# Eight modulation blocks as 1024 columns of four row groups instead of 512 columns of eight, in a one-core transformer trunk

## The chip, the cores and the metric

One Trainium2 (trn2) chip, one of its cores. The metric is the device time of one execution in microseconds (us). The engines are named as in the profile: PE is TensorE (the matmuls; PEld its weight loads), DVE is VectorE, ACT is ScalarE, POOL is GpSimd, SP is SyncE, whose queue issues most of the transfers. SPq and ACTq are the transfer-issuing instructions of SP and ACT.

## The reference

One layer of a streaming encoder on 512 tokens of 1024 channels, all float32. The change touches only the first line of it:

```python
mod = silu(c) @ w_ada + b_ada                 # c: 1 x 1024, w_ada: 1024 x 6144
sh1, sc1, g1, sh2, sc2, g2 = split(mod, 6)    # six rows of 1024
h = rms_norm(x) * (1 + sc1) + sh1
proj = h @ w_in                               # 1024 x 1696
gm  = gmlp(proj[:, :1024])                    # u and v halves, v is layer-normed and mixed over positions
mla = attention(proj[:, 1024:])               # q and kv latents (672 columns), 8 heads
x = x + g1 * (concat(rms_norm(gm), rms_norm(mla)) @ w_out)
x = x + g2 * moe(rms_norm(x) * (1 + sc2) + sh2)   # 64 experts, top 8, and a shared one
```

## The kernel before, in words

There is no planner. Each engine has its own program, written out in order, and engines wait for each other on semaphores that count completed steps. Tokens are worked on in four tiles of 128 (t = 0 to 3); the 1024 channels are eight row groups of 128 (c = 0 to 7).

**The modulation.** `w_ada` is 24 MB, twelve blocks of 2 MB. Partition p holds rows 8p to 8p+7 of it, so one block is eight multiply-adds of DVE (a column of `silu(c)` times a row group, added to an accumulator), after which a matmul with a matrix of ones on PE sums the accumulator over the 128 partitions (`ada_sum`, L611) and ACT copies the sum from its PSUM bank into the row `mod` (`copy_mod`, L1000). The first four blocks (`first_block`, L1322) make `sh1` and `sc1`. They are already cut as 1024 columns of four row groups, and are summed differently, into columns. The other eight (`ada_block`, L1375) are 512 columns of all eight row groups; two of them make one row of `mod`. These eight are numbered 0 to 7 in what follows, and the four rows of `mod` that they make (gate 1, shift 2, scale 2, gate 2) are rows 0 to 3. Rows of `mod` are used only from the scaling of `w_out` on (L519) and later. But PE waits once for all eight copies ahead of the up-projections (L675), ACT waits for all eight blocks ahead of its latent casts (L1087), POOL ahead of its key copies (L513), and SP ahead of the load of `w_u` (L419), since memory is shared.

**The order around it.** From about 40 us to 120 us the engines run side by side:

- PE (L647 to L671): the latent projections, two to a tile of tokens (512 and 160 columns; eight accumulating matmuls each), then the v projections, one of 512 columns to a tile, then 20 transposes of the latents. The eight `ada_sum` stand among them: one behind the first projection of tiles 1, 2 and 3, one behind the last latent projection, and one behind each of the four v projections. Projection i waits until the result of projection i-4 has been copied out of its bank (L633: `proj_ok` at least i-3, i counted from 0; so the seventh, i = 6, needs the third copy).
- ACT (L1050 to L1088): the copies of these results, `copy_mod` behind the same projections, ten small loads that it issues itself behind tile 0 (`load_smalls`, L1033), the scaling of the latents, casts of the weights to reduced precision (L1072), GELU of v, the casts `latT_high`.
- DVE (L1400 to L1433): block 0, then for each tile one block and the squares of the tile's latents (`lat_sums`, L1391), then blocks 5 to 7, the low parts of the weights (L1414), statistics of v, and `latT_low` (L1431), for which PE waits at L674.
- SP (L407 to L420): the load of each block waits until the block that used its buffer three blocks ago is done (L410). A load of 2 KB of `b_ada` follows each. `w_v`, `w_q`, `w_kv` are loaded in between.
- An accumulator may be written again when PE has summed it (L1380), a bank when ACT has copied it (L616).

From 120 us on come the up-projections, attention, the output projection, routing, and from about 340 us the 64 experts, which take two thirds of the time and which the change doesn't touch.

Of the kernel before, what the change touches and what calls it, by code (L numbers as in the profile page):

```python
# [46 lines left out]
def trunk_kernel(nc, a, out):  # L47
# [31 lines left out]
    with ExitStack() as ctx:  # L79
# [20 lines left out]
        w_lat = at("w_lat_sb", 72, [P, C, LAT])  # L100
        ada_w = [at(f"ada_w{i}", kb, [P, C, BANK]) for i, kb in enumerate((94, 110, 40))]
        h = at("h_sb", 126, [P, T, D])
# [3 lines left out]
        acc_g1 = at("acc_g1", 28, [P, D])  # L106
        bias0 = [at(f"bias0_{i}", kb, [P, BANK]) for i, kb in enumerate((163, 165, 16))]
        u = at("u_sb", 16, [P, T, GW])
# [112 lines left out]
        cact = small("cact", [P, C])  # L221
        acc = [small(f"ada_acc{i}", [P, BANK]) for i in range(3)]
        ss = small("ss", [P, T])
# [9 lines left out]
        ws_raw = small("ws_raw", [P, GG, GB])  # L233
        lsq = at("lsq", 18, [P, QL])
        ws_low = small("ws_low", [P, GG, GB])
# [119 lines left out]
        def ada_buffer(j):  # L355

            n = j - ADA_FIRST
            return n % 3, 32 * (n // 3 + 1) + 16

# [32 lines left out]
        def _(sp):  # L392
# [14 lines left out]
            for j in range(ADA_FIRST, ADA):  # L407
                i, _ = ada_buffer(j)

                sp.wait_ge(ada_dve, (1, 2, 4)[i] if j < ADA_FIRST + 3 else j - 2)  # L410
                sp.dma_start(ada_w[i][:], w_ada_v[:, :, j * BANK:(j + 1) * BANK]).then_inc(ld_ada[i], 16)
                sp.dma_start(bias0[i][0:1, :], a["b_ada"][:, j * BANK:(j + 1) * BANK]).then_inc(ld_ada[i], 16)
                if j == ADA_FIRST + 2:
                    sp.dma_start(w_v[:], w_in_v[:, :, GW:2 * GW]).then_inc(ld["wv"], 16)
                if j == ADA_FIRST + 4:
                    sp.wait_ge(hT_tr, 2 * T)
                    sp.dma_start(w_q[:], a["w_q_up"][0].rearrange("(p c) n -> p c n", c=QC)).then_inc(ld["wq"], 16)
                    sp.dma_start(w_kv[:], a["w_kv_up"][0].rearrange("(p c) n -> p c n", c=KC)).then_inc(ld["wq"], 16)
# [69 lines left out]
        def _(pool):  # L488
# [15 lines left out]
            pool.memset(bias0[0][:], 0.0)  # L504
            pool.memset(bias0[1][:], 0.0)
            pool.memset(bias0[2][:], 0.0).then_inc(bias_zero, 1)
            pool.wait_ge(ld["ws"], 16)
# [87 lines left out]
        def _(pe):  # L595
# [14 lines left out]

            def ada_sum(j):  # L611

                n = j - ADA_FIRST
                pe.wait_ge(acc_ok, n + 1)
                if n >= 2:
                    pe.wait_ge(mod_ok, n - 1)  # L616
                pe.matmul(bank[j % 2][:], ones[:], acc[n % 3][:], start=True, stop=True).then_inc(ada_mm, 1)

# [30 lines left out]
            for t in range(T):  # L649
                for m, (n0, n1) in enumerate(lat_cuts):  # L650
                    projection(t * NL + m, t, w_lat, n0, n1)
                    if t and m == 0:
                        ada_sum(ADA_FIRST + t - 1)
                if t == 2:
# [3 lines left out]
                    last.then_inc(wsT_tr, 1)  # L658
            ada_sum(ADA_FIRST + T - 1)
            pe.wait_ge(ld["wv"], 16)  # L660
            for t in range(T):
                projection(V0 + t, t, w_v, 0, GW)
                ada_sum(ADA_FIRST + T + t)

# [325 lines left out]
        def _(act):  # L990
# [8 lines left out]

            def copy_mod(j):  # L1000
                act.wait_ge(ada_mm, j - ADA_FIRST + 1)
                act.copy(mod[:, j // 2, j % 2 * BANK:(j % 2 + 1) * BANK], bank[j % 2][:]).then_inc(mod_ok, 1)

# [46 lines left out]
            for t in range(T):  # L1050
                for m, (n0, n1) in enumerate(lat_cuts):
                    i = t * NL + m
                    act.wait_ge(proj_mm, i + 1)
                    act.copy(lat[:, t, n0:n1], bank[2 + i % 4][:, 0:n1 - n0]).then_inc(proj_ok, 1)
                    if t and m == 0:
                        copy_mod(ADA_FIRST + t - 1)
                if t == 0:
                    load_smalls()
            copy_mod(ADA_FIRST + T - 1)
            act.wait_ge(stats_ok, 1)  # L1060
# [17 lines left out]
            for t in range(T):  # L1078
                gelu(v, V0 + t, t)
                copy_mod(ADA_FIRST + T + t)  # L1080

# [230 lines left out]
        def _(dve):  # L1312
# [62 lines left out]
            def ada_block(j):  # L1375
                n = j - ADA_FIRST
                buf, loads = ada_buffer(j)
                dve.wait_ge(ld_ada[buf], loads)
                if n >= 3:
                    dve.wait_ge(ada_mm, n - 2)  # L1380
                w = ada_w[buf]
                link(dve.scalar_tensor_tensor(acc[n % 3][:], w[:, 0, :], cact[:, 0:1], bias0[buf][:], ALU.mult, ALU.add))
                for c in range(1, C):
                    ins = dve.scalar_tensor_tensor(acc[n % 3][:], w[:, c, :], cact[:, c:c + 1], acc[n % 3][:], ALU.mult, ALU.add)
                    if c < C - 1:
                        link(ins)
                ins.then_inc(acc_ok, 1)
                dve.wait_ge(acc_ok, n + 1)
                dve.engine_nop().then_inc(ada_dve, 1)
# [410 lines left out]
```

## Time and profile before

| | |
|---|---|
| three runs | 1049.43, 1050.78 (median), 1052.73 us |
| the profiled execution | 1044.55 us, of which the span of its trace is 1042.7 us |
| mean granted clock of PE | 0.975 of full speed |
| busy, share of the span | PE 90%, DVE 84%, ACT 59%, POOL 30% |
| instructions | 14345, of which DVE 1306 |
| q1 (SP's transfers) | 73344 packets, 252.23 MB |
| q10 (ACT's transfers) | 4064 packets, 0.94 MB |

The profile is of one execution. "Busy" counts the time in which an engine has an instruction in work. Idle time ahead of an instruction is given with what ended it (the releaser); "issue" stands where the engine waited for nothing that the profile shows. The chain of waits is the work that ended last, followed back from the end.

### The profile page before, as it was taken

The page shows a single profiled execution, that of the slowest core. Times are in us where ns is not written, and L with a number is a line of the kernel's source. Part 1 is how long each engine was busy: PE and PEld are TensorE (multiplying, and loading weights), DVE is VectorE, ACT ScalarE, POOL GpSimd, SP SyncE. Part 2 cuts the span into 40 slices and gives each one's busy share as a digit, 9 for nine tenths or more (in the row PEclk, how much of TensorE's full clock was granted, in tenths as well). Part 3 has the DMA queues.
Part 4 walks back from the last instruction along what each step waited for, and adds up shares of the span by engine and source line. Part 5 has one row for each costly group of instructions (what it writes and reads, how often), then busy time and mean ns, then how long its engine had stood idle before and what let it go on. Part 6 is the DMA issues. An engine that isn't in the chain of part 4 may idle for free.

```text
span 1042.7 us, 14345 instructions
## 1 busy us (share of the span) xinstructions
PE 940.5 (90%) x4323; PEld 734.3 (70%) x4324; DVE 870.9 (84%) x1306; ACT 612.0 (59%) x969; POOL 316.3 (30%) x193
## 2 busy tenths in 40 slices
PE   1899999899998989989999999999999999889984
PEld 1654674678897567778777777777777777777773
DVE  4888883456668379989999999999899999899895
ACT  4215462563041467767777777777776767677671
POOL 1000206980001123333433424333323243332422
PEclk9899999899999989999999999999999999999997
DMA  9996220202194989999999999999999999999972
GB/s 350 397 375 234 81 81 1 111 1 82 60 337 164 271 248 349 377 356 320 349 351 353 361 346 366 354 359 346 326 363 329 320 374 352 366 348 366 339 251 28
DMA packets 96497, 290.46 MB, mean 279 GB/s; under 512 B 20520, under 2 KB 21032, under 8 KB 95824
## 3 DMA queue, kind: packets, MB, share of 16 engines
q1 hardware_dynamic: 73344, 252.23, 64.5%
q0 software_dynamic: 19056, 36.89, 14.9%
q10 hardware_dynamic: 4064, 0.94, 0.4%
q8 instruction: 16, 0.26, 0.1%
q14 instruction: 17, 0.14, 0.0%
HBM read 284.60 MB, written 39.98 MB: 311 GB/s over the span
## 4 chain that ended last, share of the span: by engine, by line
DMA 38%; PE 33%; DVE 13%; issue 9%; ACT 4%; POOL 2%; POOLq 0%; SPq 0%; DVEq 0%; ACTq 0%
DMA out<-oute,src_tab 23%; DMA xe<-h_rows,src_tab 9%; PE bank L637 6%; PE bank L598 5%; PE bank L600 5%; PE bank L599 5%; DMA w_gu<-in_w_exp_up 4%; DVE gu_low L1626 3%; PE bank L710 3%; POOL out L553 2%; PE bank L879 2%; DVE oute L1662 2%; PE bank L753 2%; PE bank L863 1%; PE bank L770 1%
## 5 line engine op out<-in xcount | busy, mean ns | idle before, releaser
L1626 DVE TENSOR_TENSOR gu_low<-w_gu,gu_high 128x1024 fp32r<-128x1024 f32 x256 | 301.3, 1219 | 17.3 <-ACT gu_high L1209 13.7
L1209 ACT CAST gu_high<-w_gu 128x1024 fp32r<-128x1024 f32 x256 | 256.5, 1055 | 63.7 <-PE bank L600 42.4
L553 POOL DMA_INDIRECT out<-oute,src_tab x64 | 135.8, 2122 | 419.0 <-DMA out<-oute,src_tab 255.5
L598 PE MATMUL bank<-gu_high,xeT_high 128*128 128x512 f32 x512 | 207.4, 405 | 3.7 <-DVE xeT_low L1626 3.6
L600 PE MATMUL bank<-gu_high,xeT_low 128*128 128x512 f32 x512 | 201.5, 394 | 0.0
L599 PE MATMUL bank<-gu_low,xeT_high 128*128 128x512 f32 x512 | 201.1, 393 | 0.0
L1626 DVE TENSOR_TENSOR d_low<-w_d,d_high 128x1024 fp32r<-128x1024 f32 x128 | 150.5, 1217 | 1.8 <-ACT d_high L1215 1.8
L1215 ACT CAST d_high<-w_d 128x1024 fp32r<-128x1024 f32 x128 | 128.2, 1054 | 14.5 <-PE bank L600 11.5
L598 PE MATMUL bank<-d_high,hwT_high 128*128 128x512 f32 x256 | 109.6, 428 | 7.8 <-DVE hwT_low L1626 7.8
L598 PEld LDWEIGHTS bank<-gu_high,xeT_high 128*128 128x128 f32 x512 | 96.6, 189 | 26.0 <-issue 5.8
L600 PEld LDWEIGHTS bank<-gu_high,xeT_low 128*128 128x128 f32 x512 | 96.3, 188 | 22.3
L547 POOL DMA_INDIRECT xe<-h_rows,src_tab x64 | 98.7, 1542 | 43.4 <-DVE src_tab L1696 19.2
L599 PEld LDWEIGHTS bank<-gu_low,xeT_high 128*128 128x128 f32 x512 | 96.5, 188 | 19.5
L879 PE MATMUL bank<-ident,xe 128*128 128x128 f32 x512 | 72.9, 287 | 38.7 <-DMA xe<-h_rows,src_tab 38.4
L879 PEld LDWEIGHTS bank<-ident,xe 128*128 128x128 f32 x512 | 65.3, 194 | 56.4 <-issue 50.8
L600 PE MATMUL bank<-d_high,hwT_low 128*128 128x512 f32 x256 | 104.1, 407 | 0.0
L1626 DVE TENSOR_TENSOR xeT_low<-bank,xeT_high 128x512 fp32r<-128x512 f32 x128 | 82.1, 683 | 25.6 <-ACT xeT_high L1225 25.3
L599 PE MATMUL bank<-d_low,hwT_high 128*128 128x512 f32 x256 | 103.2, 403 | 0.0
L1225 ACT CAST xeT_high<-bank 128x512 fp32r<-128x512 f32 x128 | 68.9, 591 | 46.4 <-PE bank L879 46.4
L1662 DVE TENSOR_TENSOR oute<-bank,mod_rows 128x512 f32<-128x512 f32 x128 | 82.1, 683 | 9.4 <-PE bank L600 9.4
L598 PEld LDWEIGHTS bank<-d_high,hwT_high 128*128 128x128 f32 x256 | 50.6, 198 | 16.9 <-issue 5.1
L600 PEld LDWEIGHTS bank<-d_high,hwT_low 128*128 128x128 f32 x256 | 50.0, 195 | 11.7
(284 smaller groups left out, 1289.6 us busy)
## 6 DMA issues: line engine op xcount, KB each, us to landing
w_gu<-in_w_exp_gate SPq DMA_DIRECT2D x128, 512.0 KB, 6.2
w_gu<-in_w_exp_up SPq DMA_DIRECT2D x128, 512.0 KB, 11.2
w_d<-in_w_exp_down SPq DMA_DIRECT2D x128, 512.0 KB, 7.5
ada_w<-in_w_ada SPq DMA_DIRECT2D x8, 2048.0 KB
first_w<-in_w_ada SPq DMA_DIRECT2D x3, 2048.0 KB, 22.8
w_out_sb<-in_w_out SPq DMA_DIRECT2D x2, 2048.0 KB, 7.6
w_lat_sb<-in_w_in SPq DMA_DIRECT2D x1, 2688.0 KB, 23.2
x_sb<-in_x SPq DMA_DIRECT2D x1, 2048.0 KB, 13.7
```

The costliest lines, as they stand in the source:

```text
L547: pool.indirect_dma_start(xe[i][:], None, h2_dram, bass.IndirectOffsetOnAxis(ap=rows, axis=0), bounds_check=last_row, oob_is_err=False).th ...
L553: pool.indirect_dma_start(out_rows, bass.IndirectOffsetOnAxis(ap=rows, axis=0), oute[i][:], None, bounds_check=last_row, oob_is_err=False, ...
L598: pe.matmul(dst, xh, wh, start=start, stop=False)
L599: pe.matmul(dst, xh, wl, start=False, stop=False)
L600: return pe.matmul(dst, xl, wh, start=False, stop=stop)
L637: last = pe.matmul(bank[2 + i % 4][:, 0:n1 - n0], hT[:, c, t * P:(t + 1) * P], w[:, c, n0:n1], start=(c == 0), stop=(c == C - 1))
L879: last = pe.transpose(bank[c // 4][:, c % 4 * P:(c % 4 + 1) * P], xe[b][:, c:D:C], ident[:])
L1209: act.copy(gu_high[half][:, m], w_gu[half][i][:, m]).then_inc(gu_high_ok[half], 1)
L1215: act.copy(d_high[:, m], w_d[i][:, m]).then_inc(d_high_ok, 1)
L1225: act.copy(xeT_high[i][:, m * HC:(m + 1) * HC, :], bank[m][:].rearrange("p (c n) -> p c n", c=HC)).then_inc(xe_high_ok, 1)
L1626: return dve.tensor_tensor(low, whole, high.bitcast(F32), ALU.subtract)
L1662: last = dve.tensor_tensor(oute[i][:, cols], bank[4 + m][:], mod[:, GATE2, cols], ALU.mult)
```

## The change

Blocks 0 to 7 become 1024 columns of four row groups. Blocks 2r and 2r+1 are the two halves of the sum for row r of `mod`, in one accumulator of 1024 columns. A row of `b_ada` comes with the even block. Per block, DVE has four multiply-adds on 128x1024 in place of eight on 128x512. Each load of 2 MB reads runs of 4 KB in place of 2 KB. PE sums a whole row at once (`ada_sums(r)`: two matmuls, one for each 512 columns, into banks 0 and 1), and ACT copies it with two copies. The eight sums stand at four places in place of eight: behind the first projection of tile 2, behind the last latent projection, and behind the v projections of tiles 1 and 3. The accumulators move to the first 8 KB of each partition, where `x` was, and the small tensors behind them move down by 6 KB.

The diff (buffers and functions whole, nothing else was changed):

```diff
--- before.py
+++ after.py
@@ -98,13 +98,14 @@
         w_u = at("w_u_sb", 40, [P, C, GW])
         w_v = at("w_v_sb", 56, [P, C, GW])
         w_lat = at("w_lat_sb", 72, [P, C, LAT])
-        ada_w = [at(f"ada_w{i}", kb, [P, C, BANK]) for i, kb in enumerate((94, 110, 40))]
+        ada_w = [at(f"ada_w{i}", kb, [P, HK, D]) for i, kb in enumerate((94, 110, 40))]
         h = at("h_sb", 126, [P, T, D])
         hT = at("hT", 143, [P, C, S])
         first_w = [at(f"first_w{i}", kb, [P, HK, D]) for i, kb in enumerate((94, 110, 167, 40))]
         acc_sh1 = at("acc_sh1", 159, [P, D])
         acc_g1 = at("acc_g1", 28, [P, D])
-        bias0 = [at(f"bias0_{i}", kb, [P, BANK]) for i, kb in enumerate((163, 165, 16))]
+        bias0 = [at(f"bias0_{i}", kb, [P, D]) for i, kb in enumerate((163, 16))]
+        acc = [at(f"ada_acc{i}", 4 * i, [P, D]) for i in range(2)]
         u = at("u_sb", 16, [P, T, GW])
         v = at("v_sb", 167, [P, T, GW])
         vn = at("vn_sb", 175, [P, T, GW])
@@ -219,7 +220,6 @@
         freq = small("freq", [P, RH])
         cT = small("cT", [P, C])
         cact = small("cact", [P, C])
-        acc = [small(f"ada_acc{i}", [P, BANK]) for i in range(3)]
         ss = small("ss", [P, T])
         lnst = small("lnst", [P, T * GG, 6])
         lnmv = small("lnmv", [P, T * GG, 2])
@@ -231,7 +231,7 @@
         ln_g = small("ln_g", [P, GW])
         ln_b = small("ln_b", [P, GW])
         ws_raw = small("ws_raw", [P, GG, GB])
-        lsq = at("lsq", 18, [P, QL])
+        lsq = at("lsq", 20, [P, QL])
         ws_low = small("ws_low", [P, GG, GB])
         bsT = small("bsT", [P, GG])
         qa_g = small("qa_g", [P, QC])
@@ -355,7 +355,7 @@
         def ada_buffer(j):
 
             n = j - ADA_FIRST
-            return n % 3, 32 * (n // 3 + 1) + 16
+            return n % 3, 16 + sum(16 + 16 * (b % 2 == 0) for b in range(n % 3, n + 1, 3))
 
         def shared_banks(t):
 
@@ -408,8 +408,10 @@
                 i, _ = ada_buffer(j)
 
                 sp.wait_ge(ada_dve, (1, 2, 4)[i] if j < ADA_FIRST + 3 else j - 2)
-                sp.dma_start(ada_w[i][:], w_ada_v[:, :, j * BANK:(j + 1) * BANK]).then_inc(ld_ada[i], 16)
-                sp.dma_start(bias0[i][0:1, :], a["b_ada"][:, j * BANK:(j + 1) * BANK]).then_inc(ld_ada[i], 16)
+                s, k0 = divmod(j, 2)
+                sp.dma_start(ada_w[i][:], w_ada_v[:, k0 * HK:(k0 + 1) * HK, s * D:(s + 1) * D]).then_inc(ld_ada[i], 16)
+                if k0 == 0:
+                    sp.dma_start(bias0[s % 2][0:1, :], a["b_ada"][:, s * D:(s + 1) * D]).then_inc(ld_ada[i], 16)
                 if j == ADA_FIRST + 2:
                     sp.dma_start(w_v[:], w_in_v[:, :, GW:2 * GW]).then_inc(ld["wv"], 16)
                 if j == ADA_FIRST + 4:
@@ -502,8 +504,7 @@
             pool.iota(part[:], pattern=[[0, 1]], base=0, channel_multiplier=1, allow_small_or_imprecise_dtypes=True).then_inc(consts, 1)
 
             pool.memset(bias0[0][:], 0.0)
-            pool.memset(bias0[1][:], 0.0)
-            pool.memset(bias0[2][:], 0.0).then_inc(bias_zero, 1)
+            pool.memset(bias0[1][:], 0.0).then_inc(bias_zero, 1)
             pool.wait_ge(ld["ws"], 16)
             pool.affine_select(out=ws_low[:], in_=ws_raw[:], compare_op=ALU.is_ge, fill=0.0, base=0, pattern=[[0, GG], [-1, GB]], channel_multiplier=1).then_inc(consts, 1)
 
@@ -608,13 +609,12 @@
                     last = pe.matmul(bank[s][:, c:c + 1], acc_s[:, c::C], ones[:, 0:1], start=True, stop=True)
                 last.then_inc(col_mm, 1)
 
-            def ada_sum(j):
-
-                n = j - ADA_FIRST
-                pe.wait_ge(acc_ok, n + 1)
-                if n >= 2:
-                    pe.wait_ge(mod_ok, n - 1)
-                pe.matmul(bank[j % 2][:], ones[:], acc[n % 3][:], start=True, stop=True).then_inc(ada_mm, 1)
+            def ada_sums(r):
+                pe.wait_ge(acc_ok, r + 1)
+                for m in range(2):
+                    if r:
+                        pe.wait_ge(mod_ok, 2 * r + m - 1)
+                    pe.matmul(bank[m][:], ones[:], acc[r % 2][:, m * BANK:(m + 1) * BANK], start=True, stop=True).then_inc(ada_mm, 1)
 
             def h_transposes(t):
                 pe.wait_ge(h_ok, t + 1)
@@ -649,18 +649,19 @@
             for t in range(T):
                 for m, (n0, n1) in enumerate(lat_cuts):
                     projection(t * NL + m, t, w_lat, n0, n1)
-                    if t and m == 0:
-                        ada_sum(ADA_FIRST + t - 1)
+                    if t == 2 and m == 0:
+                        ada_sums(0)
                 if t == 2:
                     pe.wait_ge(consts, 11)
                     for g in range(GG):
                         last = pe.transpose(bank[6][:, g * GB:(g + 1) * GB], ws_low[:, g, :], ident[:])
                     last.then_inc(wsT_tr, 1)
-            ada_sum(ADA_FIRST + T - 1)
+            ada_sums(1)
             pe.wait_ge(ld["wv"], 16)
             for t in range(T):
                 projection(V0 + t, t, w_v, 0, GW)
-                ada_sum(ADA_FIRST + T + t)
+                if t % 2:
+                    ada_sums(2 + t // 2)
 
             pe.wait_ge(latn_ok, 1)
             pe.wait_ge(proj_ok, V0 + T)
@@ -997,9 +998,10 @@
             act.wait_ge(ld["c"], 16)
             act.activation(cact[:], cT[:], ACT.Silu).then_inc(silu_c, 1)
 
-            def copy_mod(j):
-                act.wait_ge(ada_mm, j - ADA_FIRST + 1)
-                act.copy(mod[:, j // 2, j % 2 * BANK:(j % 2 + 1) * BANK], bank[j % 2][:]).then_inc(mod_ok, 1)
+            def copy_mod(r):
+                for m in range(2):
+                    act.wait_ge(ada_mm, 2 * r + m + 1)
+                    act.copy(mod[:, 2 + r, m * BANK:(m + 1) * BANK], bank[m][:]).then_inc(mod_ok, 1)
 
             act.wait_ge(ld["x"], 16)
             for t in range(T):
@@ -1052,11 +1054,11 @@
                     i = t * NL + m
                     act.wait_ge(proj_mm, i + 1)
                     act.copy(lat[:, t, n0:n1], bank[2 + i % 4][:, 0:n1 - n0]).then_inc(proj_ok, 1)
-                    if t and m == 0:
-                        copy_mod(ADA_FIRST + t - 1)
+                    if t == 2 and m == 0:
+                        copy_mod(0)
                 if t == 0:
                     load_smalls()
-            copy_mod(ADA_FIRST + T - 1)
+            copy_mod(1)
             act.wait_ge(stats_ok, 1)
             act.activation(latss[:, :, 0], latss[:, :, 0], ACT.Sqrt, bias=epsc[:], scale=1.0 / QL).then_inc(lstd_ok, 1)
             act.activation(latss[:, :, 1], latss[:, :, 1], ACT.Sqrt, bias=epsc[:], scale=1.0 / KL).then_inc(lstd_ok, 1)
@@ -1077,7 +1079,8 @@
 
             for t in range(T):
                 gelu(v, V0 + t, t)
-                copy_mod(ADA_FIRST + T + t)
+                if t % 2:
+                    copy_mod(2 + t // 2)
 
             for c in range(QC + KC):
                 act.wait_ge(latT_tr, c + 1)
@@ -1373,19 +1376,22 @@
                 dve.tensor_scalar(hT[:, c, :], hT[:, c, :], g1_col[:, c:c + 1], sh1_col[:, c:c + 1], ALU.mult, ALU.add).then_inc(hT_ok, 1)
 
             def ada_block(j):
-                n = j - ADA_FIRST
+                r, k0 = divmod(j - ADA_FIRST, 2)
                 buf, loads = ada_buffer(j)
                 dve.wait_ge(ld_ada[buf], loads)
-                if n >= 3:
-                    dve.wait_ge(ada_mm, n - 2)
-                w = ada_w[buf]
-                link(dve.scalar_tensor_tensor(acc[n % 3][:], w[:, 0, :], cact[:, 0:1], bias0[buf][:], ALU.mult, ALU.add))
-                for c in range(1, C):
-                    ins = dve.scalar_tensor_tensor(acc[n % 3][:], w[:, c, :], cact[:, c:c + 1], acc[n % 3][:], ALU.mult, ALU.add)
-                    if c < C - 1:
+                if r >= 2 and k0 == 0:
+                    dve.wait_ge(ada_mm, 2 * r - 2)
+                w, acc_r = ada_w[buf], acc[r % 2]
+                for c in range(HK):
+                    kc = k0 * HK + c
+                    ins = dve.scalar_tensor_tensor(acc_r[:], w[:, c, :], cact[:, kc:kc + 1], acc_r[:] if kc else bias0[r % 2][:], ALU.mult, ALU.add)
+                    if c < HK - 1:
                         link(ins)
-                ins.then_inc(acc_ok, 1)
-                dve.wait_ge(acc_ok, n + 1)
+                if k0:
+                    ins.then_inc(acc_ok, 1)
+                    dve.wait_ge(acc_ok, r + 1)
+                else:
+                    link(ins)
                 dve.engine_nop().then_inc(ada_dve, 1)
 
             def lat_sums(t):
```

## Rows read from the trace of the kernel before

**Rows 1.** Windows of the stretch 60 to 90 us (window, us, busy of each engine, clock)

```profile
60.00:90.00 30.00, 30.00 (x107) 17.17 (x106) 24.33 (x41) 10.28 (x22) 0.64 (x1) 1.00 1.06 377
```

**Rows 2.** The chain of waits, 59 to 119 us (start, us, engine, tile, line)

```profile
59.46 0.86 PE bank L617 x2
60.31 9.04 PE bank L637 x32
...
72.39 0.44 PE bank L657 x4
...
83.58 6.87 PE bank L637 x16
...
114.48 2.48 PE bank L670 x20
116.96 2.39 issue
```

**Rows 3.** Who waited for whom, 40 to 112 us: the sums of PE

```profile
PEld bank L617 <- DVE ada_acc L1384: 0.2, 1, 0.2
```

**Rows 4.** Timeline of DVE, 40 to 122 us

```profile
44.76 0.75 DVE L1382 SCALAR_TENSOR_TENSOR ada_acc<-ada_w,cact,bias 128x512 f32<-128x512 f32 x1
45.54 5.48 DVE L1384 SCALAR_TENSOR_TENSOR ada_acc<-ada_w,cact,ada_acc 128x512 f32<-128x512 f32 x7
...
67.38 0.56 DVE L1393 CUSTOM_DVE_ANT_0 lsq<-lat_sb 128x384 f32<-128x384 f32 x1 [2.31 <-ACT lat_sb L1054]
...
69.24 5.48 DVE L1384 SCALAR_TENSOR_TENSOR ada_acc<-ada_w,cact,ada_acc 128x512 f32<-128x512 f32 x7
...
86.90 5.48 DVE L1384 SCALAR_TENSOR_TENSOR ada_acc<-ada_w,cact,ada_acc 128x512 f32<-128x512 f32 x7
...
99.66 5.48 DVE L1384 SCALAR_TENSOR_TENSOR ada_acc<-ada_w,cact,ada_acc 128x512 f32<-128x512 f32 x7
...
115.86 2.07 DVE L1431 SCALAR_TENSOR_TENSOR latT_low<-bank,qa_g,latT_high 128x512 fp32r<-128x512 f32 x3 [1.93 <-ACT latT_high L1088]
117.85 1.40 DVE L1431 SCALAR_TENSOR_TENSOR latT_low<-bank,kva_g,latT_high 128x512 fp32r<-128x512 f32 x2
```

**Rows 5.** Timeline of DVE at 21 us: a block of the other shape

```profile
21.38 5.22 DVE L1335 SCALAR_TENSOR_TENSOR acc_sh<-first_w,cact,acc_sh 128x1024 f32<-128x1024 f32 x4
```

**Rows 6.** Timeline of ACT, its queue and POOL, 52 to 118 us

```profile
52.63 0.39 ACTq L1034 DMA_DIRECT2D ws_raw<-in_gm_ws  x1
...
60.24 5.80 ACTq L1048 DMA_DIRECT2D rbias<-in_router_bias  x1
60.74 0.64 POOL L508 TENSOR_SCALAR_AFFINE_SELECT ws_low<-ws_raw 128x512 f32<-128x512 f32 x1 [56.47 <-DMA ws_raw<-in_gm_ws]
...
66.08 0.58 ACT L1054 COPY lat_sb<-bank 128x512 f32<-128x512 f32 x1 [13.16 <-issue]
...
114.52 0.59 ACT L1002 COPY mod_rows<-bank 128x512 f32<-128x512 f32 x1 [0.26 <-PE bank L617]
115.14 1.84 ACT L1088 ACTIVATE latT_high<-bank,qa_g 128x512 fp32r<-128x512 f32 x3
```

**Rows 7.** DMA, 60 to 66 us: packets, MB, share of the 16 engines

```profile
q1 hardware_dynamic: 828, 1.67, 77.4%
q10 hardware_dynamic: 828, 0.53, 30.1%
```

**Rows 8.** DMA, 70 to 80 us

```profile
q1 hardware_dynamic: 1068, 3.79, 98.0%
q10 hardware_dynamic: 1067, 0.03, 7.6%
```

**Rows 9.** DMA, 12 to 22 us (4 KB runs) and 40 to 50 us (2 KB runs)

```profile
DMA packets 1045, 4.15 MB, mean 415 GB/s; under 512 B 32, under 2 KB 32, under 8 KB 1045
...
DMA packets 1911, 3.86 MB, mean 386 GB/s; under 512 B 34, under 2 KB 34, under 8 KB 1909
```

**Rows 10.** DMA, 90 to 98 us: GB/s in 40 slices

```profile
GB/s 369 410 369 399 399 348 410 389 379 389 389 379 399 379 389 399 369 379 328 246 215 143 102 51 41 10 0 0 0 0 0 0 0 0 0 0 0 0 0 0
```

## Prediction

> **What bounds the kernel now.** I read the windows first, to see which engine is full where the changed code runs. From 60 to 90 us PE is busy for 30.00 of 30 us and DVE for 24.33 [rows 1]: PE has no gap to give. The chain of waits says the same in order of time. From 59.46 to 116.96 us it stays on PE throughout, through latent projections, sums, v projections and transposes, each piece beginning where the last one ends [rows 2]. PE then stands still for 2.39 us, up to about 119.35. The timeline of DVE names what it waits for: the last `latT_low` ends at 117.85 + 1.40 = 119.25 [rows 4], and L674 wants it. That handoff is PE's transposes, ACT's casts from 115.14, DVE's low parts from 115.86 [rows 4, 6]. Last I looked at the waits, for the one path by which the modulation could hold PE: PE's weight loads waited for the accumulator once, for 0.2 us [rows 3]. So here the end is set by PE's own work and by the handoff at 115 to 119 us. DVE's blocks lie beside it.
>
> **Part by part.**
>
> *The multiply-adds (DVE).* A block is one operation of 0.75 us and seven that take 5.48, from 44.76 to 51.02: 6.26 us [rows 4]. The new shape is in the trace already: four operations on 128x1024 take 5.22 us [rows 5]. That saves 1.04 us a block, 8.3 us for eight. The Trainium skill says of this (VectorE: DVE Perf Modes, "The DRAIN you can't avoid" and its rules) that every operation has a flush of its own and that one should minimise the number of operations; by that rule this is the right edit, and the trace agrees on the size. Whether it reaches the end is another matter.
>
> *When the sums are ready against when PE asks.* From PE's pieces [rows 2] the new order can be laid out. Behind the first projection of tile 1, at 59.46, no sum stands any more. The next 9.04 us are the second projection of tile 1 and the first of tile 2, up to 68.50; two sums, 1.72, up to 70.22; the second projection of tile 2, 9.04 - 6.87 = 2.17, up to 72.39; the four transposes of `ws_low`, 0.44, up to 72.83; tile 3, 9.04, up to 81.87; sums, up to 83.59; two v projections of 6.87, up to 97.33; sums, up to 99.05; two more, up to 112.79; sums, up to 114.51. Before, the transposes begin at 114.48. It is the same eight sums of 0.86 us in the same stretch, so this costs PE nothing as long as no sum waits. The row r of 1024 needs both of its blocks, so each first sum now depends on a block later than before:
>
> - Row 0 is asked for at 68.50. Even at the old speed block 1 would end at 44.76 + 2 x 6.3 = 57.4.
> - Row 1, asked for at 81.87, needs block 3. In the old trace this ends at 69.24 + 5.48 = 74.72 [rows 4], and with 1.04 less at 73.7. Cover 8.2 us.
> - Row 2, asked for at 97.33, needs block 5, old end 92.38, new about 91.3. Cover 6.0 us, the thinnest.
> - Row 3, asked for at 112.79, needs block 7. Blocks 5, 6 and 7 from 86.15 take 3 x 5.26, so it ends at about 101.9 (old 105.14). Cover 10.9 us.
>
> All four covers hold without the faster operations. The saving therefore turns into idle time of DVE ahead of 115.86, where it waits for ACT anyhow [rows 4]. DVE's work from there on is chained to `latT_low`, so nothing of the saving gets past it. SP, POOL and ACT wait for the last block too (`w_u`, the key copies, the casts). They get it about 3 us earlier, and none of the three is in the chain. Counted at nothing.
>
> *The last handoff.* ACT's chain before is `mod` copy at 114.52, 0.59, then casts from 115.14 [rows 6]. After, GELU of the fourth v tile comes one sum earlier, and two copies follow; the second waits for the sum that ends where the old last one did, so the casts start at 115.1 again. I take 0. If both copies fell behind the last sum, it would be one copy more, +0.6 us. If the transposes started sooner because GELU ends sooner, the gain is bounded by 0.1 us, since the matmuls before them end at 114.48.
>
> *New waits.* Block 4 may overwrite the accumulator only after row 0 is summed (70.22) and starts at about 76 to 78. Block 6 needs row 1 summed (83.59) and starts at 91.4. The sums for row r need the copies of row r-1, which ACT makes 10 us or more ahead. All at nothing, with these margins as the cover.
>
> *The loads.* Bytes stay the same. Runs of 4 KB moved at 415 GB/s and runs of 2 KB at 386 [rows 9], so 2 MB take some 0.4 us less, 3 us in all. The last load ended by about 96 us [rows 10], and its block wasn't asked for by PE until 112.8. If the blocks now catch up with the loads, DVE waits, not PE. The eight `b_ada` loads become four on SP's queue, which shortens a queue nobody waits for. POOL's two wider clears in place of three lie at 4 us, where SP needs them at 17: nothing.
>
> *ACT's small loads, the one cost I can't read off.* ACT issues ten loads from 52.63 on and is held in the last for 5.80 us, to 66.04; only then does it copy the latents of tile 1, from 66.08 [rows 6]. The copy ends at 66.66, and PE wants it at 72.83 for the first projection of tile 3: a margin of 6.2 us. What holds ACT is how fast its packets leave. The rows show equal numbers from both queues: 828 and 828 in 6 us, 1068 and 1067 in 10 us [rows 7, 8]. So each small packet waits out one of SP's. At 2 KB a packet that is 138 a microsecond for each queue, at 3.5 KB (3.79 MB over 1068) it is 107. With 4 KB packets ahead, the 828 of that stretch take 7.8 us in place of 6: ACT is free some 2 us later, at 68. Lower bound 0; upper bound, if the whole 13.4 us of issuing doubled, 13.4. I take 2, since rows 8 are the nearest to the new size, and that is within the margin: cost 0, bounds 0 and 13.4 - 6.2 = 7.2 us. `ws_low` has more room (ready at 61.38, wanted at 72.39). Block 3 would start 2 us later too, and its cover falls from 8.2 to 5.9. The Trainium skill (DMA: Bandwidth & Descriptors, "Queues, rings and completion order") says that an engine takes turns between queues packet by packet. It speaks against the change: larger runs on one queue slow the small ones of the other. The equal counts agree.
>
> *Sum:* 0 us on the path, with bounds of -0.1 and +0.6 for the handoff. The working is against the profiled execution of 1044.55 us, which lies 0.6% below the median of 1050.78. As the difference is nil, the forecast is that median.
>
> **The rivals.**
>
> *DVE's time counts after all (faster).* If the 8.3 us went through, by a wait on the blocks which the trace doesn't name, the time would be 1042.5. For it: DVE is 81% busy in this window, and it is just behind its loads. Against: one wait of 0.2 us in all, and 8 us of cover. The VectorE page's rule, taken as a rule for the kernel's time, would give the same number. Chance 0.04.
>
> *ACT's issuing reaches PE (slower).* Place: PE's wait at L633 ahead of tile 3, at 72.83. It decides from the point where ACT is free later than 72.2, which is 6.2 us later than now. Price: the delay less 6.2, so 7.2 us at the upper bound, 1058.0; a delay of 9.4 gives the 3.2 us that can be told from nothing. DVE's `lat_sums(1)` and block 3 would slip with it, but their cover is as large. For it: the turn-taking of the queues. Against: the rate at 3.5 KB, which gives 2 us. Chance 0.05.
>
> *The change saves no DVE time* (the new block as long as the old). Then nothing else moves either and the time is 1050.8. This can't be told apart by the time, only by the rows. Chance 0.02, counted with "no change".
>
> *Something outside this stretch.* The two thirds of the time in the experts have a chain that runs through transfers, and the small tensors move in memory. The work there is untouched, but three runs of one kernel spread over 3.3 us. I leave 0.05 on the faster side and 0.06 on the slower.
>
> **How the numbers follow.** 0.3% of the time, 3.2 us, is about what a measurement of this kernel can tell from no change. "Same" gets the forecast and the third rival, 0.80. Faster gets 0.04 + 0.05 = 0.09, slower 0.05 + 0.06 = 0.11. The predicted time is 1050.8. The range is that value, the handoff's bounds, the spread of the runs before (1049.43 to 1052.73) for a second median, and part of the slower rival: 1047.2 to 1054.6.
>
> **What would show it.** Right: `ada_acc` operations of 1.28 us, 32 of them in place of 64, DVE's busy time down by about 8 us and none of it in the span; the chain on PE from 59 to 117 us with the sums in pairs at about 68.5, 81.9, 97.3 and 112.8; the transposes at 114.5 and the first up-projection at 119.4 again; ACT's last issue ending at about 68. Wrong: a wait of PE on `ada_acc` at row 1 or 2, a gap of PE at 72.8 that ends with ACT's copy, or an up-projection that starts a microsecond or more off 119.4. A changed median with the first up-projection at 119.4 would mean a cause outside this stretch.

## The result and the profile after

| | before | after |
|---|---|---|
| median of nine runs | 1049.43 us (1044.64 to 1054.74) | 1061.05 us (1054.31 to 1064.77) |
| ratio, 95% interval | | 1.0098 (1.0071 to 1.0126) |
| the profiled execution, its span | 1044.55, 1042.7 us | 1064.36, 1062.5 us |
| DVE busy, instructions | 870.9 us, 1306 | 864.7 us, 1274 |
| packets of SP's queue (q1) | 73344 | 69240 |
| PE's first up-projection | 119.35 us | 128.06 us |

The changed kernel is slower by 1%, some 10 us (7 to 13 by the interval). The prediction said no change. Line numbers after 220 of the changed kernel differ by a few from those before.

The chain of waits of the changed kernel in the same stretch (start, us, engine, tile, line) no longer stays on PE [rows 2]:

```profile
41.86 11.67 PE bank L637 x32
53.98 0.52 ACTq L1050
...
56.05 3.69 ACTq L1050
...
65.06 12.95 ACTq L1050
78.05 0.59 ACT lat_sb L1056
78.69 12.03 PE bank L637 x32
90.71 1.72 PE bank L617 x4
92.43 13.73 PE bank L637 x32
106.16 1.72 PE bank L617 x4
107.88 13.73 PE bank L637 x32
121.61 1.72 PE bank L617 x4
123.33 2.36 PE bank L671 x20
125.69 2.37 issue
```

It runs through ACT's queue, to the last of the ten small loads, which now holds ACT for 12.95 us in place of 5.80 [rows 6]. The sums stand in pairs of 1.72 as laid out, and none of them waits. The timelines of ACT's queue and ACT, and that of PE, show both ends of the wait:

```profile
65.06 12.95 ACTq L1050 DMA_DIRECT2D rbias<-in_router_bias  x1
78.05 1.27 ACT L1056 COPY lat_sb<-bank 128x512 f32<-128x512 f32 x3 [24.21 <-issue]
```

```profile
73.14 0.60 PE L657 MATMUL bank<-ident,ws_low 128*128 128x128 f32 x4
78.69 12.03 PE L637 MATMUL bank<-w_lat_sb,hT 128*128 128x512 f32 x32 [4.94 <-ACT lat_sb L1056]
```

ACT is free at 78.01 instead of 66.04, its copy of the latents of tile 1 is late, and PE stands still for 4.94 us ahead of tile 3. Then the same two projections that took 9.04 us [rows 2] take 12.03. (A row that begins behind a gap counts 0.17 us more than one in an unbroken row; read in the same way, in e1 below, the two take 9.21.) The windows of the changed kernel say why (window, us, busy of PE, PEld, DVE, ACT, POOL, granted clock, DMA share, GB/s):

```profile
74.00:79.00 5.00, 0.31 (x1) 0.32 (x2) 0.14 (x1) 0.95 (x3) 0.00 (x0) 0.84 1.03 392
79.00:83.00 4.00, 4.00 (x5) 1.53 (x5) 3.86 (x7) 1.50 (x4) 0.00 (x0) 0.50 0.64 178
83.00:87.00 4.00, 4.00 (x9) 1.78 (x8) 3.85 (x8) 0.00 (x0) 0.00 (x0) 0.85 0.19 29
87.00:91.00 4.00, 4.00 (x22) 2.95 (x21) 3.89 (x4) 0.84 (x2) 0.00 (x0) 1.00 0.97 371
```

The granted clock falls while PE still stands (0.84 in the first row), and after the gap PE is granted half its clock (0.50, 1.2 instead of 2.4 GHz) until about 84 us. So the first up-projection is 8.71 us late, and that adds up from rows: 0.06 in the start, 0.86 because the first three projections ran longer on half clock (18.52 against 17.66), 4.94 of waiting, 2.99 in the two projections afterwards (2.82 of it half clock, 12.03 against 9.21), less 0.14 in the transposes and the last handoff. The 0.86 isn't the change's: in the four experiments whose code is that of the kernel before up to there, these projections took 17.72, 18.50, 18.77 and 19.11 us.

The timeline of DVE of the changed kernel shows that its own part went as meant:

```profile
46.13 9.21 DVE L1387 SCALAR_TENSOR_TENSOR ada_acc<-ada_w,cact,ada_acc 128x1024 f32<-128x1024 f32 x7
...
78.86 0.56 DVE L1399 CUSTOM_DVE_ANT_0 lsq<-lat_sb 128x384 f32<-128x384 f32 x1 [17.16 <-ACT lat_sb L1056]
...
124.58 2.07 DVE L1437 SCALAR_TENSOR_TENSOR latT_low<-bank,qa_g,latT_high 128x512 fp32r<-128x512 f32 x3 [4.93 <-ACT latT_high L1091]
```

Two blocks take 10.5 us instead of 12.5. Over all eight the `ada_acc` operations keep DVE busy for 41.0 us instead of 48.5, and its whole busy time falls by 6.2 us, somewhat less than the 8 that the prediction named. DVE then waits 17.16 us for ACT, and again 4.93 us ahead of `latT_low` (1.93 before, [rows 4]).

The cause is to be seen in the DMA queues. First the changed kernel from 58 to 68 us and from 68 to 78 us, packets, MB, share:

```profile
q1 hardware_dynamic: 802, 3.21, 81.1%
q10 hardware_dynamic: 799, 0.76, 22.6%
...
q1 hardware_dynamic: 736, 3.99, 99.1%
q10 hardware_dynamic: 738, 0.01, 4.5%
```

Then the kernel before, 60 to 70 us:

```profile
q1 hardware_dynamic: 1484, 3.00, 83.6%
q10 hardware_dynamic: 1484, 0.63, 24.4%
```

Equal numbers of packets leave the two queues in both kernels, as if they took turns. With 2 KB packets on SP's queue 148 of ACT's packets leave in a microsecond, with 4 KB packets 80. From 68 on there are 5.4 KB to a packet (3.99 MB over 736), since `w_q` and `w_kv` come in, and it is 74. SP issues `w_q` 6 us earlier than before; its queue after, and before:

```profile
56.24 0.35 SPq L419 DMA_DIRECT2D w_q_sb<-in_w_q_up  x1
...
62.23 1.31 SPq L417 DMA_DIRECT2D w_q_sb<-in_w_q_up  x1
```

### The profile page after: what moved, and what is told of

It reads as the page before. It is cut to its first block, busy times and chain, and to the rows that moved or that the text cites. A ratio compares the mean times of both kernels' runs of the same rounds, so it can differ in the third digit from the quotient of the medians.

```text
span 1062.5 us, 14303 instructions
## 1 busy us (share of the span) xinstructions
PE 943.8 (89%) x4323; PEld 736.0 (69%) x4324; DVE 864.7 (81%) x1274; ACT 613.4 (58%) x969; POOL 320.1 (30%) x192
## 3 DMA queue, kind: packets, MB, share of 16 engines
q1 hardware_dynamic: 69240, 252.23, 64.0%
q10 hardware_dynamic: 4064, 0.94, 0.4%
## 4 chain that ended last, share of the span: by engine, by line
DMA 47%; PE 32%; DVE 7%; issue 7%; ACT 3%; ACTq 2%; POOL 1%; POOLq 0%; SPq 0%; DVEq 0%
DMA out<-oute,src_tab 40%; DMA xe<-h_rows,src_tab 6%; PE bank L637 5%; PE bank L599 4%; PE bank L601 4%; PE bank L600 4%; PE bank L711 3%; ACTq L1050 2%; DVE gu_low L1632 2%; PE bank L754 1%; PE bank L864 1%; POOL out L554 1%; DVE oute L1668 1%; PE bank L771 1%; DMA x_sb<-in_x 1%
## 5 line engine op out<-in xcount | busy, mean ns | idle before, releaser
L554 POOL DMA_INDIRECT out<-oute,src_tab x64 | 143.3, 2239 | 427.1 <-DMA out<-oute,src_tab 313.6
L548 POOL DMA_INDIRECT xe<-h_rows,src_tab x64 | 94.6, 1479 | 43.1 <-DVE src_tab L1702 19.1
```

The costliest lines, as they stand in the source:

```text
L548: pool.indirect_dma_start(xe[i][:], None, h2_dram, bass.IndirectOffsetOnAxis(ap=rows, axis=0), bounds_check=last_row, oob_is_err=False).th ...
L554: pool.indirect_dma_start(out_rows, bass.IndirectOffsetOnAxis(ap=rows, axis=0), oute[i][:], None, bounds_check=last_row, oob_is_err=False, ...
```

## The experiments

Eight experiments ran, two of them (e4 and e7) with the same kernel. All ratios are to the kernel before, timed on the same chips.

**e1_smalls_late.** The changed kernel, with nine of the ten small loads issued behind the first GELU of v:

```diff
@@ load_smalls, and its call behind tile 0
-                act.dma_start(ws_raw[:], ...).then_inc(ld["ws"], 16)
...
                 if t == 0:
-                    load_smalls()
+                    act.dma_start(ws_raw[:], ...).then_inc(ld["ws"], 16)
@@ the v loop of ACT
                 gelu(v, V0 + t, t)
+                if t == 0:
+                    load_smalls()
```

> The changed kernel with nine of ACT's ten small loads moved from behind tile 0 to behind the first GELU of v, when SP's loads are nearly through; ws_raw stays. Theory A (ACT's issuing, held back by the large packets of SP's queue, makes PE wait at tile 3, and PE then runs at half clock for a while: 4.9 + 3.0 us): ACT copies the latents of tile 1 right behind the projection, PE has no gap at 73 to 79 us, the first up-projection comes at 119 to 120 us instead of 128.1, and the time is that of the kernel before within 0.3%, 8 to 9 us below the changed kernel. Rival B (the pairs of sums, or the accumulator in place of x, or something in the expert stage cost the time): still 8 to 10 us above the kernel before. Rival C (both: only part of the 10 us is the wait): between, 2 to 4 us above the kernel before.

Measured: 1048.45 us, ratio 0.9992 (0.9961 to 1.0023). The first up-projection comes at 120.73 us, 0.7 later than expected, since PE began 0.5 us later than in the kernel before and its first three projections took 18.63 us. PE's timeline has no gap at tile 3, and the projections take 9.2 us:

```profile
73.74 0.60 PE L657 MATMUL bank<-ident,ws_low 128*128 128x128 f32 x4
74.17 9.21 PE L637 MATMUL bank<-w_lat_sb,hT 128*128 128x512 f32 x32
```

The whole loss is gone with ACT's wait, the rest of the change being in. Theory A holds; sums in pairs, accumulators in place of `x` and moved tensors cost nothing that can be told, to some 3 us.

**e2_runs_2kb.** The changed kernel with each block's load in two halves, so that packets are 2 KB again:

```diff
-                sp.dma_start(ada_w[i][:], w_ada_v[:, k0 * HK:(k0 + 1) * HK, s * D:(s + 1) * D]).then_inc(ld_ada[i], 16)
+                for m in range(2):
+                    sp.dma_start(ada_w[i][:, :, m * BANK:(m + 1) * BANK], w_ada_v[:, k0 * HK:(k0 + 1) * HK, s * D + m * BANK:s * D + (m + 1) * BANK]).then_inc(ld_ada[i], 16)
```

> The changed kernel with each 2 MB load cut into two loads of 512 columns each, so that SP's packets are 2 KB again; operations of DVE, sums and copies stay as in the changed kernel. Theory A, in the form that the size of SP's packets is what holds ACT: ACT's last issue ends at about 66 us as before, no gap of PE, first up-projection at about 119.5 us, time within 0.3% of the kernel before. Rival B (sums in pairs, DVE or memory layout): 8 to 10 us above it. Rival D (what holds ACT is that SP runs ahead and brings the packets of w_q and w_kv among the small ones, not the size of the blocks' own): ACT's last issue still ends at 70 us or later.

Measured: 1048.05 us, ratio 0.9998 (0.9963 to 1.0033). ACT's last issue is as in the kernel before:

```profile
61.86 5.71 ACTq L1051 DMA_DIRECT2D rbias<-in_router_bias  x1
67.61 0.78 ACT L1057 COPY lat_sb<-bank 128x512 f32<-128x512 f32 x2 [13.03 <-issue]
```

It ends at 67.57; tile 0 was 1.7 us late in this run, and the first up-projection comes at 120.88. What holds ACT is thus the size of SP's packets, and nothing else in the change. That includes SP running ahead: with packets of 2 KB, and DVE as fast as in the changed kernel, `w_q` is issued at 62.77 us again.

**e3_before_act_12us.** The kernel before with only ACT's lateness put in:

```diff
                 if t == 0:
                     load_smalls()
+                    for i in range(11):
+                        act.copy(x[:, 2], x[:, 0]).then_inc(idle_ok, 1)
+                        act.wait_ge(idle_ok, i + 1)
```

> The kernel before with 12 us of copies on ACT (11 of 128x1024, x to a part of x that nothing reads again) behind its small loads, so that the latents of tile 1 are copied at about 78 us as in the changed kernel. No other part of the change is in it. Theory A: PE waits some 5 us ahead of tile 3 and runs the next 3 to 4 us of work at half clock, first up-projection at about 127.5 us, time 8 us (0.8%) above the kernel before. Rival B: the late copy costs PE little, 0 to 3 us. If the gap costs 5 us but no half clock follows, 5 us above.

Measured: 1058.41 us (only four runs), ratio 1.0102 (1.0037 to 1.0167); first up-projection at 127.49. Its timelines of ACT and PE:

```profile
66.15 11.81 ACT L1061 COPY x_sb<-x_sb 128x1024 f32<-128x1024 f32 x11 [13.15 <-issue]
...
78.63 9.06 PE L638 MATMUL bank<-w_lat_sb,hT 128*128 128x512 f32 x16 [5.73 <-ACT lat_sb L1055]
```

The lateness alone gives the loss of the change, as closely as four runs can tell: 5.73 us of gap, and 9.06 us for a projection that takes 7.03 at full clock.

**e4_before_smalls_late and e7_before_smalls_again.** The kernel before with the nine loads moved as in e1; the second is the same kernel once more.

> The kernel before with the nine small loads moved as in e1. Theory A: in the kernel before ACT is free in time anyway, so the move is worth nothing: first up-projection at 119.4 us, time within 0.3% of the kernel before. If the move alone gains 2 us or more, then the likeness of e1 and the kernel before would not show that the wait is the whole cost.

Measured: 1045.69 us, ratio 0.9950 (0.9916 to 0.9984), outside what was expected, although the first up-projection came at 120.31 us, no earlier than before.

> e4 once more, since it measured 0.5% below the kernel before (interval 0.9916 to 0.9984) although its trace has the first up-projection no earlier (120.3 against 119.4 us). If there is a gain outside this stretch, the ratio is 0.993 to 0.998 again. If it was chance, it lies at 0.998 to 1.002, as it did for e1, which has the same move on the changed kernel.

Measured: 1052.60 us, ratio 1.0009 (0.9974 to 1.0044). The gain of e4 didn't come again, so I take it for chance. The move itself is worth nothing that can be told in the kernel before, so the recovery in e1 is the wait's; e2 and e5 recover as much with all ten loads in their old place.

**e5_wq_later.** The changed kernel with `w_q` and `w_kv` loaded two blocks later (`if j == ADA_FIRST + 6` in place of `+ 4` in SP's loop).

> The changed kernel with the loads of w_q and w_kv issued two blocks later, so that their packets (7 KB on average at 70 to 74 us) don't stand among ACT's small ones. In the changed kernel 209 of ACT's packets left from 70 to 74 us, against about 87 a microsecond beside 4 KB packets. Theory A1 (the blocks' own 4 KB packets do nearly all of it): ACT is free at 76 to 77 us instead of 78.0, PE still waits 2.5 to 4 us ahead of tile 3 and half clock follows; time 0.6 to 1.0% above the kernel before. Theory D (the large packets of w_q and w_kv do a good part): ACT is free by 74 us, PE's wait is under 1 us, time within 0.3% of the kernel before.

Measured: 1050.71 us, ratio 1.0013 (0.9979 to 1.0047); first up-projection at 120.68. The timelines of ACT's queue and PE:

```profile
64.08 9.27 ACTq L1050 DMA_DIRECT2D rbias<-in_router_bias  x1
...
74.03 9.31 PE L637 MATMUL bank<-w_lat_sb,hT 128*128 128x512 f32 x32 [1.14 <-ACT lat_sb L1056]
```

ACT is free at 73.35. That is nearer theory D than A1, though PE's wait of 1.14 us is a little over D's; it is what the prediction's deciding point of 72.2 us gives. From its first small load to the end of its last one ACT takes 13.41 us in the kernel before, 20.65 here and 24.45 in the changed kernel (which also began 0.93 us later). So the blocks' own packets make 7.2 us of it and those of `w_q` and `w_kv` 3.8. In the kernel before the latter came after ACT was free: up to 70 us SP's packets are of 2.0 KB there. What held ACT's packets back shows at the end of this run too. From 74 to 76 us SP's queue ran dry: 116 of its packets left in these 2 us, and 1324 of ACT's. The packet size was necessary (e2), but without the two it costs PE 1.1 us, and no half clock follows: 9.31 us for what took 9.21 in e1.

**e6_before_act_7us.** e3 with seven copies instead of eleven.

> The kernel before with seven in place of eleven copies on ACT (7.5 us), so that the copy of tile 1 ends at about 74.3 us and PE waits only about 1.5 us ahead of tile 3. If the half clock comes with any wait of PE, this costs 1.5 + 3 = 4.5 us (first up-projection at 123.5 to 124 us, 0.4% above the kernel before). If it takes a longer wait such as the 4.9 and 5.7 us seen so far, it costs 1.5 us (first up-projection at about 121 us, no difference that can be told).

Measured: 1055.40 us, ratio 1.0031 (0.9997 to 1.0065), which doesn't rule out no change; first up-projection at 124.01, which looks like the first case. The rows say otherwise. PE's timeline:

```profile
75.15 7.13 PE L638 MATMUL bank<-w_lat_sb,hT 128*128 128x512 f32 x16 [1.48 <-ACT lat_sb L1055]
...
124.01 0.66 PE L599 MATMUL bank<-w_q_high,latT_high 128*128 128x384 f32 x1 [4.44 <-issue]
```

After 1.48 us PE kept its clock (7.13 against 7.03). Of the 4.66 us, 0.8 is half clock at the start, 1.7 the gap, and 2.1 stand in the last handoff, 4.44 in place of 2.39. The timeline of DVE names it:

```profile
119.39 0.84 DVE L1423 BATCH_NORM_STATS2 lnst<-v_sb 128x6 f32<-128x128 f32 x4
120.26 0.38 DVE L1426 BATCH_NORM_AGGREGATE lnmv<-lnst 128x2 f32<-128x6 f32 x4
120.55 2.04 DVE L1435 SCALAR_TENSOR_TENSOR latT_low<-bank,qa_g,latT_high 128x512 fp32r<-128x512 f32 x3
```

`latT_low` follows the statistics without idle time: with blocks of the old shape DVE, made late by `lat_sums(1)`, sets the end. In e5, where the blocks are the new ones and PE waits about as little, DVE still waited 3.34 us for ACT there, and the handoff took 2.42 us. So the saving of DVE was not wholly idle: beside a short wait of PE it kept a second loss of some 2 us off. Beside the long one it matters little: in e3, with blocks of the old shape and PE itself 8 us late, the handoff took 2.52 us, 0.13 more than before.

**e8_one_load_late.** The changed kernel with one load, `on_g` (1024 packets of 4 bytes), moved behind the first GELU.

> The changed kernel with only one of the ten small loads moved behind the first GELU of v: on_g, the one of 1024 packets of 4 bytes. Theory A, in the form that ACT is held because a certain number of packets may be under way: the nine others bring 2080 packets in place of 3100, the last issue isn't held for 13 us any more, ACT is free by 68 us, PE has no gap, first up-projection at 119.5 to 121 us, time within 0.3% of the kernel before. If ACT is held by something else (time from issue to landing of each load, for one), it is still free only at 74 us or later and PE waits.

Measured: 1051.75 us, ratio 1.0000 (0.9972 to 1.0028); first up-projection at 119.83. ACT's queue:

```profile
55.74 3.75 ACTq L1049 DMA_DIRECT2D kva_g<-in_kv_a_g  x1
...
62.89 1.88 ACTq L1049 DMA_DIRECT2D rbias<-in_router_bias  x1
64.82 0.78 ACT L1055 COPY lat_sb<-bank 128x512 f32<-128x512 f32 x2 [11.28 <-issue]
```

The hold at `kva_g` is that of the changed kernel (3.75 us against 3.69), but nothing is held at the end. Of the edits tried this is the smallest that takes the loss away. No kernel that ran is faster than the kernel before, e4's unrepeated gain aside; there as here PE has no gap from 42 us to its last handoff. This fits a queue in which only so many packets may be under way. When the last issue was through, 1359 of ACT's packets had left since 54 us in the kernel before, 1346 in e2, 1509 in e5 and 1599 after the change, out of some 3100 (4064 less the 960 of the first 12 us). That leaves 1500 to 1750 waiting each time; in e8 it is 653 out of 2060, some 1400. The four numbers aren't one number, so a plain limit on packets is not shown, and the limit itself was not tried.

## Why the prediction was wrong

Most steps held. The block took 5.25 us, as the rows of the other shape said; the sums in pairs cost PE nothing and came in the order laid out; the four covers were enough even with DVE 10 us late, the thinnest being row 1, ready at 85.2 us and asked for at 90.7; the handoff of 2.37 us and the new waits cost nothing, and no block waited for its load; the transposes gained the 0.1 us of the bound. The rival that DVE's time counts fell: in e1 too, with ACT's wait gone, the time is that of the kernel before and not 8 us below it.

The step that failed is "ACT's small loads", counted at 0 with a delay of 2 us. Mechanism, place and deciding point of the slower rival were right: ACT free later than 72.2 us, PE waiting ahead of tile 3. What was wrong were two sizes, and one thing was overlooked.

- *How many packets.* I took the 828 of the last 6 us. But every packet since ACT began was slower, and the last issue ended only when about 1350 had left (1509 in e5, 1599 after the change).
- *The rate.* I took 107 a microsecond from the stretch of 70 to 80 us, as "3.5 KB a packet" [rows 8]. That mean mixed packets of 2 KB with those of `w_q` and `w_kv`, and 3.5 isn't 4: beside packets of 4 KB, ACT's packets of a few bytes left at 97 a microsecond (579 in e5 from 66 to 72 us). And ACT's own packets were small only in that stretch. From 58 to 68 us of the changed kernel they carry 0.76 MB over 799, about 1 KB each, which shares the same 397 GB/s, and it is 80. By these numbers 1359 packets at 80 take 17 us, so from 56.5 us ACT would be free at 73.5, and e5 has 73.35; but that it fits so closely is luck, since in e5 it was 1509 packets at 87. The rate fell to nearly half (80 against 148), and the time of issuing grew from 13.41 to 20.65 us. My own upper bound of 13.4 us held; I chose the value by the wrong nearest row.
- *What else comes in.* With half as many packets to a block SP's issuing was held less and ran ahead: `w_q` was issued at 56.2 us instead of 62.2 (62.8 in e2, with packets of 2 KB). Their large packets then stood among ACT's small ones, for 3.8 us more. I had called a shorter queue of SP one that nobody waits for.

Together 11.0 us, and 12.0 with ACT's later start, against the 2 of the sum. The price was short as well: delay less 6.2 is 5.8 us, or 4.94 as PE itself was 0.9 late, and I left out the slower work that followed, 2.99 us, nearly all of it half clock. With it the rival's price would have been some 8 to 9 us and its time 1059. It also should have had far more than 0.05: that an engine takes turns between queues packet by packet, as the Trainium skill says (DMA: Bandwidth & Descriptors, "Queues, rings and completion order"), was cited as speaking against the change, and then overruled by a mean. The runs agree with it, with 799 against 802 packets.

The trace shows 8.7 us up to the first up-projection, the runs 10 (7 to 13). The stretch from there on differs between runs of the same code: from one point ahead of the experts (329.24 us before, 337.76 after, so 8.5 us apart) to the end of the span it is 713 us in the profile before, but 717 in e7 and 725 in e6, which have its code there; and 725 after, but 714 in e5 and e8 and 724 in e1, which have the changed code. So what the profiles differ by behind that point can't be put down to the change.

## What to carry to other kernels

Here larger packets gained a little for the transfer itself (415 against 386 GB/s [rows 9]) and slowed the small transfers on the other queue, packet for packet; so count the small packets under way, and look for what the engine that issues them has to do next. For the rate, look for a stretch in which all the neighbour's packets have the new size and your own have theirs, not for a mean. And price a new wait of PE with the clock that it may be granted afterwards: here 5 us of standing still cost 8.

## What was not expected of the hardware

After gaps of 4.94 and 5.73 us PE ran on half clock, for 2.82 and 2.03 us more in the work behind; after gaps of 1.14 and 1.48 us it did not. The length of the gap alone doesn't decide it. The last handoff is a gap of 2.4 us in nearly every run, and behind it the granted clock differs. First e1, then e8, both with a gap of 2.42 us:

```profile
121.00:125.00 4.00, 4.00 (x23) 3.83 (x22) 3.86 (x24) 1.27 (x3) 0.00 (x0) 1.00 0.00 0
...
121.00:125.00 4.00, 4.00 (x15) 3.96 (x14) 3.89 (x21) 0.95 (x3) 0.00 (x0) 0.57 0.00 0
```

The kernel before was on half clock from 120 to 123 us (0.50), and so was e4 from 122 to 125 (0.50), but not e7 (1.00), which is the same kernel as e4. What decides it stays open.

The first projections, behind the same work each time, took 17.66 to 19.11 us in runs of the same code, by how long half clock lasted (granted clock from 46 to 50 us: 1.00 before, 0.77 in e7). An issue of 128 packets on ACT's queue took 5.80 or 12.95 us, ending when some 1350 or 1600 packets had left.
